# The scan's decay products with their operands exchanged, two heads side by side, and their result turned back on TensorE

## What is computed

```
seg = a_cum[:, :, :, None] - a_cum[:, :, None]
decay = jnp.exp(jnp.where(causal, seg, -jnp.inf))
cb = jnp.einsum('bclgn,bcsgn->bclsg', cc, bc)
y_diag = jnp.einsum('bclsgh,bcsghp->bclghp', cb[..., None] * decay, xf)
...
y_off = jnp.einsum('bclgn,bcghpn->bclghp', cc, prev) * jnp.exp(a_cum)[..., None]
return (y_diag + y_off).reshape(bsz, seq, n_h, p)
```

## Time and profile before

| | us |
|---|---|
| median of 3 runs | 1999.66 (1999.62 to 2000.08) |
| the profiled execution | 2000.4 |
| its span, first to last instruction | 1998.7 |
| PE busy / DVE busy / ACT busy / POOL busy | 1994.0 / 1291.5 / 1118.5 / 192.7 |
| granted TensorE clock, all of the span | full |

### The profile page before, as it was taken

One profiled execution on the slowest core, in us unless ns is written; L12 is line 12 of the kernel. 1 busy time (PEld: TensorE's weight loads), 2 busy tenths in 40 slices (PEclk: granted clock), 3 DMA queues, 4 the chain that ended last, 5 costly groups with the idle time before them and its releaser, 6 DMA issues.

```text
span 1998.7 us, 25559 instructions
## 1 busy us (share of the span) xinstructions
PE 1994.0 (100%) x9050; PEld 1658.2 (83%) x9050; DVE 1291.5 (65%) x1509; ACT 1118.5 (56%) x1284; POOL 192.7 (10%) x191
## 2 busy tenths in 40 slices
PE   9999999999999999999999999999999999999999
PEld 8888888888888888888888888888888888888887
DVE  5777777777887666666675665656555555654564
ACT  6666666667776454556764444555445435534542
POOL 2110120112222111110000000010000000000000
PEclk9999999999999999999999999999999999999999
DMA  7777887889997666566896667767667766766764
GB/s 247 209 200 200 217 202 201 222 230 237 247 245 210 195 195 189 189 194 185 233 240 203 202 207 237 205 190 227 203 190 208 224 192 193 234 196 186 215 222 162
DMA packets 330351, 418.99 MB, mean 210 GB/s; under 512 B 145152, under 2 KB 145600, under 8 KB 330000
## 3 DMA queue, kind: packets, MB, share of 16 engines
q1 hardware_dynamic: 329344, 414.71, 72.1%
q10 hardware_dynamic: 448, 2.24, 0.3%
q0 software_dynamic: 464, 0.77, 0.2%
HBM read 382.46 MB, written 2.16 MB: 192 GB/s over the span
## 4 chain that ended last, share of the span: by engine, by line
PE 97%; issue 2%; DMA 0%; DVE 0%; ACT 0%; POOL 0%; DVEq 0%; SPq 0%; POOLq 0%; ACTq 0%
PE ps L670 31%; PE ps L672 31%; PE ps L671 31%; PE ps L848 1%; DMA k_tiles<-qk_half 0%; PE ps L618 0%; PE ps L836 0%; PE ps L682 0%; POOL rqk L2175 0%; PE ps L859 0%; PE ps L744 0%; PE ps L721 0%; DVE wlo L1499 0%; ACT whi L971 0%; PE ps L642 0%
## 5 line engine op out<-in xcount | busy, mean ns | idle before, releaser
L1499 DVE TENSOR_TENSOR wlo<-raw,whi 128x1024 fp32r<-128x1024 f32 x703 | 882.7, 1262 | 608.5 <-ACT whi L971 606.4
L971 ACT ACTIVATE whi<-raw 128x1024 fp32r<-128x1024 f32 x703 | 738.7, 1057 | 639.9 <-PE ps L672 622.5
L670 PE MATMUL ps<-whi,xT_hi 128*128 128x512 f32 x1268 | 497.0, 392 | 0.0
L672 PE MATMUL ps<-whi,xT_lo 128*128 128x512 f32 x1268 | 493.8, 389 | 0.0
L671 PE MATMUL ps<-wlo,xT_hi 128*128 128x512 f32 x1268 | 493.5, 389 | 0.0
L672 PEld LDWEIGHTS ps<-whi,xT_lo 128*128 128x128 f32 x1268 | 238.0, 188 | 50.1
L671 PEld LDWEIGHTS ps<-wlo,xT_hi 128*128 128x128 f32 x1268 | 238.2, 188 | 47.9
L670 PEld LDWEIGHTS ps<-whi,xT_hi 128*128 128x128 f32 x1268 | 238.1, 188 | 47.9 <-issue 0.2
L670 PE MATMUL ps<-whi,fT_hi 128*128 128x512 f32 x512 | 199.3, 389 | 0.0
L670 PE MATMUL ps<-whi,hT_hi 128*128 128x512 f32 x512 | 199.3, 389 | 0.0
L671 PE MATMUL ps<-wlo,fT_hi 128*128 128x512 f32 x512 | 199.2, 389 | 0.0
(11 more groups left out here) (287 smaller groups left out, 1980.4 us busy)
## 6 DMA issues: line engine op xcount, KB each, us to landing
raw<-in_w_in SPq DMA_DIRECT2D x319, 512.0 KB, 4.4
raw<-in_w_up SPq DMA_DIRECT2D x128, 512.0 KB, 4.2
raw<-in_w_down SPq DMA_DIRECT2D x128, 512.0 KB, 4.3
raw<-in_w_ssm_out SPq DMA_DIRECT2D x64, 512.0 KB, 4.1
raw<-in_w_attn_out SPq DMA_DIRECT2D x32, 512.0 KB, 4.3
raw<-in_w_out SPq DMA_DIRECT2D x32, 512.0 KB, 4.2
arow<-arows SPq DMA_DIRECT2D x16, 512.0 KB, 5.0
x_in<-in_x SPq DMA_DIRECT2D x4, 512.0 KB, 8.2
```

What stands on the lines that cost most here:

```text
L670: mm(dst, xh, whi[sl][:, kk, :], start=(s == 0 and kk == 0), stop=False)
L672: last = mm(dst, xl, whi[sl][:, kk, :], start=False, stop=(s == US - 1 and kk == UK - 1))
L971: A(whi[s % SLOTS][:, :, :], raw[s % SLOTS][:, :, :], ACT.Copy).then_inc(hi_ready, 1)
L1499: V.tensor_tensor(wlo[s % SLOTS][:, :, :], raw[s % SLOTS][:, :, :], fp(whi[s % SLOTS][:, :, :]), ALU.subtract).then_inc(lo_ready, 1)
```

## The change

1. `ssd_y` on PE exchanges its operands: xf[:, h, :] is stationary (128x64) and M[:, h, :] moving (128 columns). The result is channels x tokens; even heads go to PSUM partitions 0 to 63, odd heads to 64 to 127, so that two heads lie side by side over the same 128 columns.
2. ACT gets `y_evac`: it copies the whole bank (128x512) to a new tile `yc`, which lies in M's place. PE gets `ssd_turn`: 4 transposes of 128x128 turn yc back into PSUM bank 5, from which DVE adds it to xs.
3. The products stand behind unit 3 of the block and not behind unit 4. In even rounds the turn stands behind unit 4; in odd rounds it stands in the same place as the products, behind `ssd_off` and `ssd_cb`.
4. The decay is made ahead: `ssd_seg` of a round moves from step 0 of its block to step 6 (odd rounds) or step 5 (even rounds, behind `ssd_y`) of the block before; `ssd_exp` moves from step 2 to step 0 (round 0 keeps its step), and `ssd_M` from step 3 (step 2 in round 0) to step 1.
5. M may be written again once the turn has read yc (`y_T` in place of `y_mm`). DVE's last pass of the loop is written out, since there is no next round in it.

```diff
                     if later(n):
-                        pe.wait_ge(yd_done, n)
+                        pe.wait_ge(yc_out, n)
                     for hh in range(HG):
-                        last = mm(ps[6][:, hh * SHD:(hh + 1) * SHD], M[:, hh, :], xf[:, hh, :], start=True,
+                        d0 = hh % 2 * SHD
+                        last = mm(ps[6][d0:d0 + SHD, hh // 2 * P:(hh // 2 + 1) * P], xf[:, hh, :], M[:, hh, :], start=True,
                                   stop=True)
                     last.then_inc(y_mm, 1)
+                return f
+
+            def ssd_turn(n):
+                def f():
+                    pe.wait_ge(yc_out, n + 1)
+                    if later(n):
+                        pe.wait_ge(yd_done, n)
+                    for i in range(HG // 2):
+                        last = transpose(ps[5][:, i * P:(i + 1) * P], yc[:, i, :])
+                    last.then_inc(y_T, 1)
                 return f
...
-                first = {4: [ssd_y(n, 0, g)]}
+                first = {3: [ssd_y(n, 0, g)], 4: [ssd_turn(n)]}
...
-                       after={4: [ssd_y(n + 1, 1, g), ssd_off(n + 1, g), ssd_cb(g + 1)]})
+                       after={3: [ssd_y(n + 1, 1, g), ssd_off(n + 1, g), ssd_cb(g + 1), ssd_turn(n + 1)]})
...
+            def y_evac(n):
+                def f():
+                    act.wait_ge(y_mm, n + 1)
+                    A(yc[:, :, :].rearrange("p i l -> p (i l)"), ps[6][:, :], ACT.Copy).then_inc(yc_out, 1)
+                return f
...
-                steps(b + 2, {2: [ssd_exp(n + 2)], 3: [] if later(j) else [x_halve(11)],
-                              4: [xd_round(g + 1)], 7: [z_sigmoid(b + 2, g + 1)]})
+                steps(b + 2, {0: [ssd_exp(n + 2)], 3: [] if later(j) else [x_halve(11)],
+                              4: [xd_round(g + 1)], 7: [z_sigmoid(b + 2, g + 1)]}, early={4: [y_evac(n + 2)]})
...
                     if later(n):
-                        dve.wait_ge(y_mm, n)
+                        dve.wait_ge(y_T, n)
                     V.tensor_tensor(M[:, :, :], arow[:, :, :], over(acum[:, c, bass.ds(g * HG, HG)], 2, P),
...
-                    V.tensor_tensor(xs_at(g, c), xs_at(g, c), ps[6][:, :], ALU.add).then_inc(yd_done, 1)
+                    V.tensor_tensor(xs_at(g, c), xs_at(g, c), ps[5][:, :], ALU.add).then_inc(yd_done, 1)
```

More of the change, by code:

```diff
@@ L342, in build @@
         yd_done = sem("yd_done")
+        yc_out = sem("yc_out")
+        y_T = sem("y_T")
         yo_done = sem("yo_done")
@@ L874, in ssd_blocks @@
                 stream(b + 1, 1, 10 + 2 * j, xT_hi, xT_lo,
-                       after={4: [ssd_y(n + 1, 1, g), ssd_off(n + 1, g), ssd_cb(g + 1)]})
-                stream(b + 2, 0, 11 + 2 * j, xT_hi, xT_lo, after={4: [ssd_y(n + 2, 0, g + 1)]})
+                       after={3: [ssd_y(n + 1, 1, g), ssd_off(n + 1, g), ssd_cb(g + 1), ssd_turn(n + 1)]})
+                stream(b + 2, 0, 11 + 2 * j, xT_hi, xT_lo, after={3: [ssd_y(n + 2, 0, g + 1)], 4: [ssd_turn(n + 2)]})
                 stream(b + 3, 1, 11 + 2 * j, aT_hi, aT_lo,
-                       after={4: [ssd_y(n + 3, 1, g + 1), ssd_off(n + 3, g + 1)] + ([] if last else [ssd_cb(g + 2)])})
+                       after={3: [ssd_y(n + 3, 1, g + 1), ssd_off(n + 3, g + 1)] + ([] if last else [ssd_cb(g + 2)])
+                              + [ssd_turn(n + 3)]})
             ssd_blocks(0)
@@ L1893, in merge_attn, with ssd_blocks @@
                 return f
-            def ssd_blocks(j):
+            def ssd_blocks(j, last=False):
                 b = B_SSD + 4 * j
@@ L1905, in ssd_blocks @@
-                steps(b + 1, {0: [ssd_seg(n + 1, 1, g)], 1: [ssd_cbm(n + 1, 1, g)],
-                              2: [] if later(j) else [conv_taps(11, 0)], 3: [ssd_M(n + 1)],
-                              4: [] if later(j) else [conv_taps(11, 1)], 5: [ssd_y(n + 1, 1, g)],
+                    steps(b, {0: [ssd_seg(n, 0, g)], 1: [ssd_cbm(n, 0, g), ssd_M(n)], 4: [conv_taps(10, 1)],
+                              5: [ssd_y(n, 0, g)], 6: [x_join(9), ssd_seg(n + 1, 1, g), xd_rest(g)],
+                              7: [c_join(11), z_gate(g)]})
@@ L1908, in ssd_blocks @@
+                steps(b + 1, {1: [ssd_cbm(n + 1, 1, g), ssd_M(n + 1)],
+                              2: [] if later(j) else [conv_taps(11, 0)],
+                              4: [] if later(j) else [conv_taps(11, 1)],
+                              5: [ssd_y(n + 1, 1, g), ssd_seg(n + 2, 0, g + 1)],
                               6: [y_gated(g, 0)], 7: [y_norm(g)]})
-                steps(b + 2, {0: [ssd_seg(n + 2, 0, g + 1)], 1: [ssd_cbm(n + 2, 0, g + 1)], 3: [ssd_M(n + 2)],
+                steps(b + 2, {1: [ssd_cbm(n + 2, 0, g + 1), ssd_M(n + 2)],
@@ L1910, in ssd_blocks @@
                               4: [] if later(j) else [x_join(10)], 5: [ssd_y(n + 2, 0, g + 1)],
-                              6: [xd_rest(g + 1)], 7: [z_gate(g + 1)]})
-                steps(b + 3, {0: [ssd_seg(n + 3, 1, g + 1)], 1: [ssd_cbm(n + 3, 1, g + 1)], 3: [ssd_M(n + 3)],
-                              4: [] if later(j) else [x_join(11)], 5: [ssd_y(n + 3, 1, g + 1)],
+                              6: [ssd_seg(n + 3, 1, g + 1), xd_rest(g + 1)], 7: [z_gate(g + 1)]})
+                steps(b + 3, {1: [ssd_cbm(n + 3, 1, g + 1), ssd_M(n + 3)],
+                              4: [] if later(j) else [x_join(11)],
+                              5: [ssd_y(n + 3, 1, g + 1)] + ([] if last else [ssd_seg(n + 4, 0, g + 2)]),
@@ L1914, in ssd_blocks @@
                               6: [y_gated(g + 1, 1)], 7: [y_norm(g + 1), merge_attn(b + 3, j)]})
             ssd_blocks(0)
-            with dve.Fori(1, 4) as j:
+            with dve.Fori(1, 3) as j:
                 ssd_blocks(j)
+            ssd_blocks(3, last=True)
             def y_join(G):
```

19 lines of the change are left out of this document (9 added, 10 removed).

## The result

The changed kernel takes 2010.88 us (median of 6 runs, 2009.9 to 2012.61) against 1999.82 us (6 runs, 1999.46 to 2000.1) beside it: ratio 1.0055, 95% interval 1.0044 to 1.0066. It is slower by 11.1 us; 6.8 were forecast. The profiled execution took 2009.9 us, its span is 2008.2 us, 9.5 longer than before.

A forecast was written before the change was run, and what follows sets the result against it. The prediction took PE to bound the kernel, with 97% of the last-ending chain. PE's work of -2.9 us and waits of +9.7 us gave +6.8 us on the median 1999.66: 2006.5 us, range 1998 to 2022.5.

The forecast's parts named there:

- PE's work: Products and turn on PE: 1.17 + 0.44 - 1.79 = -0.18 us a round, -2.9 us in 16 rounds.
- round 1: PE's old wait on M of 0.3 us goes, since M no longer stands behind the convolution's taps.
- overlap of the pair: Exchanged products on PE: both heads of a pair stream at once, 8 x 0.111 + 0.28 = 1.17 us a round.
- price of the shape: Products on PE: 0.28 us paid once a round for going into the new record shape and out of it.
- Waits on M in rounds 2, 6, 10 and 14: PE at the products: M done at 718.8, wanted at 716.7, so 2.1 us in each round, 8.4 us.
- Rounds 4, 8 and 12: PE at the products, blocks with merge_attn on DVE: M 0.5 us late in each, 1.5 us in all.
- remainders that PE waits for: Sign of being wrong: waits of PE on DVE's remainders (wlo) in the changed kernel.
- Nothing for the copies: ACT's 16 copies, 0.64 us each, cost nothing as they are covered; only 0.1 us put in round 15.
- No overlap: Rival, products on PE: records pass one after another, 2.02 us a round, waits as added up; 2020.2 us, chance 0.27.
- overlap but for the loads: Rival, products on PE: other half's stationary load not hidden, 1.58 us a round; 2013.1 us, chance 0.15.
- M in time: Rival, rounds 2, 6, 10 and 14: M at 716.7, not 718.8, so no waits; 1996.5 us, chance 0.11.
- No price for the shape: Rival: M in time and no 0.28 us for the change of shape, another -4.5 us; 1992.0 us, chance 0.05.

The follow-up runs named there:

- e7: Changed kernel with seg behind the gating, the gate's sigmoid behind the next exponential, and all eight heads' products in the lower half: 2013.45 us (one run).
- e3: Changed kernel with ssd_seg in blocks of odd rounds put behind the gating of the group instead of ahead of it: 2000.86 us, ratio 1.0005.
- e11: Changed kernel with GpSimd's xd and xf of group 1 held back until VectorE's convolution passes of the last tile are over: 2011.83 us (one run).
- e12: e3 with the attention gate's sigmoid moved on ACT into step 2 of the next block, behind the roundings M waits for: 1998.12 us, ratio 0.9991.
- e8: Changed kernel with seg behind the gating, the gate behind the exponential, and ssd_off between fourth and fifth head's products in odd rounds: 2003.72 us (one run).
- e2: Kernel before, its products unexchanged without copy or turn, but at the new places with the decay made ahead: 2014.69 us, ratio 1.0077.
- e6: Changed kernel with only the attention gate's sigmoid moved on ACT behind the next block's exponential: 2007.72 us, ratio 1.0036.
- e1: Changed kernel's exchanged products, copy and turn, with everything at its old place except DVE's even-round add, one step later: 1999.12 us, ratio 0.9995.
- e9: e3 with GpSimd's xd and xf of group 1 held back until VectorE's convolution passes of the last tile are over: 2000.22 us, ratio 1.0000.
- e10: e1 with M of round 1 multiplied ahead of block 25's convolution passes instead of behind them and a remainder: 1999.43 us, ratio 0.9998.

## Why the prediction was right, and where its sizes were off

- **The direction, and its reason**, held: PE's work gets less and four waits on M take more. The forecast was 2006.5 us with a range of 1998 to 2022.5, wide because no row priced the pair; the time is 2010.88. The 4.3 us between are 0.9 of PE's work, 1.9 of block 26, 1.6 by which the median rose more than the span, 0.3 of rounds 4, 8 and 12, and 0.2 of round 1, less 0.5 of the waits on M and 0.1 of round 15.
- **PE's work**, -2.9 forecast, -2.0 measured. The overlap of the pair, called a guess, is real (e7). What was short is the price of the shape: 0.28 from the L787 records, 0.35 measured. The L787 records show 0.34 too. The prediction took 0.112 us for each of the eight records ahead of them, but the first of the eight takes only 0.055 (its successor starts at 64.31), so 0.06 us too little was left for the shape. It is -0.12 us a round and not -0.18.
- **Waits on M in rounds 2, 6, 10 and 14**, 8.4 forecast, 7.9 measured. In the prediction's clock of round 6, the gating was to start at 705.1 and M to be done at 718.8, 13.7 us later; measured 13.6. The products were to stand 11.6 us behind the gating's start; measured 11.8, the 0.09 ahead of the new shape among it. So the term holds for rounds 6, 10 and 14. That round 2 measured 2.19, near the forecast 2.1, is luck: e3 takes the decay out of that chain, and the wait of round 2 stays at 2.18; what goes there are the block's waits on remainders.
- **Rounds 4, 8 and 12**, 0.5 each and 1.5 forecast, 1.1, 0.4 and 0.3 measured, but not on M: PE stopped one unit earlier, for that unit's remainder, and M was just in time then. The sum was near by luck, the place was wrong: the step missed that everything ahead of M on DVE is late by the same amount, and PE wants the remainders of that unit first.
- **Block 26** is the term that was missing. I took round 2 as a copy of round 6. Ahead of it DVE has the convolution's passes and a collision with GpSimd that the earlier `ssd_off` starts, and ACT a silu and a further table load. The remainders that PE waits for there cost 1.9 us. The prediction had named remainders that PE waits for as a sign of being wrong, and in blocks 26, 28, 32 and 36 they are that, 3.7 us. One queue that I did not follow when I moved the group past it is GpSimd's; taking its collision away (e11) gives 0.8 us of block 26 back.
- **Nothing for the copies**: right. A weight load of PE waits 0.2 us for yc, in round 15 (forecast 0.1); between record starts it is under 0.1.
- **The median** rose 1.6 us more than the profiled span. Some 0.6 of it is that the profiled execution before stood that far over its median (2000.4 and 1999.82). The runs after spread from 2009.9 to 2012.6, and those from 2011.15 up have a mean granted clock of 0.998 to 0.999. The lapse of the last section would do that, but none of these longer runs has a trace, so this is argued and not shown.
- **The rivals.** No overlap (1.89 us in e7) and overlap but for the loads are out by the 1.02 us of the changed kernel's 16 records. "M in time" is what e12 made true; it measured 1998.12 where 1996.5 was worked out, 0.9 of the difference being PE's work. "No price for the shape" is out by the 0.35 us of the changed kernel and the 0.43 of e8.

## What to carry over

When work is moved on the engine that bounds the kernel, write down for each operand two intervals from one common event: how long its chain takes, and when it is wanted. Both move, and here the lead lost 4.8 us where the chain lost 1.95; the cure was the order of two pairs of entries in the side engines' queues, not the products. Then follow the releases in the other direction, to every engine that the moved work sets free, since an earlier start can fall on somebody's passes and be paid for there.

## What the hardware showed that I had not expected

**Two heads side by side are free; their shape isn't.** 16 float32 records of 64 stationary columns take 1.02 us alternating between the halves and 1.89 in one half. A pair starts 7 ns apart, pairs 0.109 us. Going in and out costs 0.35 us, a second time in the same round 0.43.

**A long wait can cost more than itself.** In e2, behind round 2's wait of 2.1 us:

```profile
625.56 0.63 PE L672 MATMUL ps<-whi,xT_lo 128*128 128x512 f32 x1
625.99 0.63 PE L670 MATMUL ps<-whi,xT_hi 128*128 128x512 f32 x1
```

```profile
600.00:620.00 20.00, 19.16 (x84) 1.00 0.44 131
625.00:629.00 4.00, 4.00 (x13) 0.57 0.77 256
```

Windows of 20 and 4 us: PE's busy time and count, the granted clock, then the share and GB/s of the DMA engines. The clock falls from 1.00 to 0.57 over 4 us, that is to 1.2 GHz for most of them, and stream records come every 0.427 us instead of 0.227. Such a lapse lasts 3.4 us and costs 1.6. e2 has two, behind the waits of rounds 2 and 14; e6 has one behind round 2, and e11 two, behind rounds 2 and 6. Not every such wait has one: the profiled execution of the changed kernel has four, of 1.9 to 2.2 us, and no lapse. In e1, e9, e10 and e12, whose longest wait in the scan is 1.6 us, no run had a mean clock under 1.000. What decides whether a wait brings a lapse stays open.

**DVE and GpSimd block each other by whole instructions.** A convolution pass of 255 columns comes every 0.39 us alone and every 1.18 us while GpSimd works on float32 tiles of 128x512; GpSimd's own xd takes 3.16 us instead of 1.04. By the starts of their instructions in that stretch, each waits for the other's current one, in turn. In e9 the two adds that read PSUM keep their 0.67 and 0.68 us beside GpSimd, and the add with both inputs in SBUF goes from 0.69 to 1.22. The Trainium skill (SBUF — State Buffer, SBUF: two separate sides) says that a VectorE instruction with two inputs in SBUF and a GpSimd instruction that reads SBUF lock each other out of a shared port pair; the rows agree. e9 and e11 add that pushing the one behind the other moves most of the loss and takes away only a part.
